# Four 32x32 blocks per head instead of two of 64x64 in the first levels of a triangular inverse

## The reference

```
up = jnp.einsum('bsnw,nwd->bsnd', branches, w_branch[l])
gates = jax.nn.sigmoid(gate_logits.reshape(b, s, N_BRANCH, D_MODEL))
x = x + jnp.sum(gates * up, axis=2) @ w_out[l]
```

## Time and profile before

| | |
|---|---|
| median of 3 runs | 2401.88 us |
| the runs | 2402.19, 2397.12, 2401.88 us |
| profiled execution | 2396.91 us |
| its span in the trace | 2395.1 us |
| PE busy | 2358.9 us, 98% |
| DVE, ACT, POOL busy | 989.7, 880.5, 1022.0 us |

### The profile page before, as it was taken

One profiled execution on the slowest core, in us unless ns is written; L12 is line 12 of the kernel. 1 busy time (PEld: TensorE's weight loads), 2 busy tenths in 40 slices (PEclk: granted clock), 3 DMA queues, 4 the chain that ended last, 5 costly groups with the idle time before them and its releaser, 6 DMA issues.

```text
span 2395.1 us, 35863 instructions
## 1 busy us (share of the span) xinstructions
PE 2358.9 (98%) x14266; PEld 1658.1 (69%) x14266; DVE 989.7 (41%) x1888; ACT 880.5 (37%) x1441; POOL 1022.0 (43%) x464
## 2 busy tenths in 40 slices
PE   8999999999999999999999999999999999999999
PEld 6744444444444444358889999888888889999887
DVE  5622222222222222245347865353453379653533
ACT  6411111101011101045447744544444477435443
POOL 0000000000000000028978555788889876547886
PEclk9999999999999999999999999999999999999999
DMA  8799999999999999945555433555555544335554
GB/s 300 298 429 429 429 429 429 430 430 430 430 429 430 430 430 430 428 183 194 193 178 168 136 125 120 171 190 192 190 179 192 189 156 154 127 101 182 176 192 143
DMA packets 96307, 650.92 MB, mean 272 GB/s; under 512 B 11088, under 2 KB 13560, under 8 KB 69688
## 3 DMA queue, kind: packets, MB, share of 16 engines
q1 hardware_dynamic: 96184, 649.21, 69.9%
HBM read 647.92 MB, written 1.25 MB: 271 GB/s over the span
## 4 chain that ended last, share of the span: by engine, by line
PE 87%; DMA 9%; DVE 3%; ACT 1%; issue 0%; POOL 0%; SPq 0%; DVEq 0%; ACTq 0%
PE bank L2477 22%; PE bank L924 12%; PE bank L669 11%; PE bank L671 10%; PE bank L670 10%; PE bank L925 6%; DMA ring<-in_expert_units 4%; DMA scratch<-in_expert_units 4%; PE bank L2464 4%; PE bank L2485 2%; PE bank L2828 1%; PE bank L2493 1%; PE bank L1418 1%; PE bank L1407 1%; PE bank L1364 0%
## 5 line engine op out<-in xcount | busy, mean ns | idle before, releaser
L656 POOL TENSOR_TENSOR w_lo<-raw,w_hi 128x1024 fp32r<-128x1024 f32 (+2 forms) x424 | 1010.5, 2412 | 1135.4 <-ACT w_hi L650 1135.2
L2477 PE MATMUL bank<-ring,scratch 128*64 128x512 f32 x2304 | 513.4, 596 | 8.8 <-DMA ring<-in_expert_units 8.8
L924 PE MATMUL bank<-hT_both,w_hi 128*128 128x512 f32 x1408 | 498.7, 398 | 4.5 <-DVE act_lo L1069 4.4
L650 ACT CAST w_hi<-raw 128x1024 fp32r<-128x1024 f32 (+2 forms) x424 | 421.6, 1041 | 180.2 <-PE bank L671 152.9
L925 PE MATMUL bank<-hT_both,w_lo 128*128 128x256 f32 x1408 | 395.1, 281 | 0.0
L2477 PEld LDWEIGHTS bank<-ring,scratch 128*64 128x64 f32 x2304 | 160.0, 137 | 323.2 <-issue 318.5
L924 PEld LDWEIGHTS bank<-hT_both,w_hi 128*128 128x128 f32 x1408 | 264.4, 188 | 70.7 <-DVE act_lo L1069 5.7
L2730 DVE TENSOR_TENSOR scratch<-bank,scratch 128x512 f32<-128x512 f32 x64 | 44.3, 692 | 597.8 <-PE bank L2493 593.8
L925 PEld LDWEIGHTS bank<-hT_both,w_lo 128*128 128x128 f32 x1408 | 266.0, 189 | 0.6
L2477 PE MATMUL bank<-scratch 128*64 128x512 f32 x768 | 172.3, 596 | 4.4 <-DMA scratch<-in_expert_units 3.3
L1058 DVE TENSOR_TENSOR bank<-bank,scratch 128x512 f32<-128x512 f32 x88 | 61.3, 697 | 275.0 <-PE bank L925 274.9
(11 more groups left out here) (388 smaller groups left out, 3326.9 us busy)
## 6 DMA issues: line engine op xcount, KB each, us to landing
ring<-in_expert_units SPq DMA_DIRECT2D x144, 2048.0 KB, 25.3
raw<-in_layer_halves SPq DMA_DIRECT2D x408, 512.0 KB, 3.8
scratch<-in_expert_units SPq DMA_DIRECT2D x47, 2048.0 KB, 26.3
ring<-in_first_units SPq DMA_DIRECT2D x11, 1024.0 KB, 11.0
ring<-in_ple_units SPq DMA_DIRECT2D x2, 2048.0 KB, 18.6
raw<-in_layer_halves SPq DMA_DIRECT2D x8, 424.0 KB, 3.2
raw<-in_layer_halves SPq DMA_DIRECT2D x4, 384.0 KB, 3.8
scratch<-in_expert_units SPq DMA_DIRECT2D x1, 1280.0 KB, 14.7
```

The lines of the kernel that those rows point to most:

```text
L650: k.nc.scalar.copy(k.w[0][i % SPLIT_SLOTS][:, at], k.raw[n % RAW_SLOTS][:, 0:at.stop - at.start]).then_inc(k.shared("weights_hi"), 1)
L656: k.nc.gpsimd.tensor_tensor(k.w[1][i % SPLIT_SLOTS][:, at], k.raw[n % RAW_SLOTS][:, 0:at.stop - at.start], k.w[0][i % SPLIT_SLOTS][:, at], ...
L924: nc.tensor.matmul(bank[:, :], w[0], both, start=start, stop=False)
L2477: last = nc.tensor.matmul(b[g * SL:(g + 1) * SL, :], lhsT[:, c, :], w[:, c, g, :], start=start and c == 0, stop=stop and c == 3)
```

## The change

Levels 0 to 4 need only diagonal blocks of 32x32: level 4 joins 16x16 blocks to 32x32. They now hold four such blocks per head (`BLOCK_ROWS`), as tiles of 128 partitions x 32 columns (`X_blocks`, `XT_blocks`, `P_blocks`). Level 4 writes its results block by block into the 64-column tiles, which DVE has set to zero before (`whole_zeros_dve`). Levels 5 and 6 are as they were. PE's list gets parts of the third gate's four quarters at other places: one in each of levels 1 to 5 between P and XP, one ahead of the last level, one inside it, one ahead of the tail; the tail's own five stay, and what is left (three parts) comes behind the tail.

```diff
+Q = 32
+BLOCK_ROWS = tuple(slice(r * Q, (r + 1) * Q) for r in range(4))
-def blocks_mm(nc, b, lhsT, rhs):
+def blocks_mm(nc, b, lhsT, rhs, blocks=HALF_ROWS):
+    n = P // len(blocks)
     for h in range(GH):
-        for rows in HALF_ROWS:
-            last = nc.tensor.matmul(b[rows, h * V:(h + 1) * V], lhsT(rows, h), rhs[rows, h, :], start=True, stop=True)
+        for rows in blocks:
+            last = nc.tensor.matmul(b[rows, h * n:(h + 1) * n], lhsT(rows, h), rhs[rows, h, :], start=True, stop=True)
...
-def level_pe(k, pe, lev):
+def level_operands(G, lev):
+    if lev < LEVELS - 2:
+        return G.X_blocks, G.XT_blocks, G.P_blocks, BLOCK_ROWS
+    return G.X, G.XT, G.P, HALF_ROWS
+
+def level_pe(k, pe, lev, fill):
     G, nc = Gdn(k), k.nc
+    X, XT, Pm, blocks = level_operands(G, lev)
     for t in range(NT):
         b, full = k.claim(pe, ("P", lev, t))
         k.evacuated(pe, ("X", t) if lev == 1 else ("XP", lev - 1, t))
-        blocks_mm(nc, b, lambda rows, h: G.m[rows, t, h, rows], G.X[:, t]).then_inc(full, 1)
+        blocks_mm(nc, b, lambda rows, h: G.m[rows, t, h, rows], X[:, t], blocks).then_inc(full, 1)
+    fill(1)
     for t in range(NT):
...
-def last_level_pe(k, pe):
+def last_level_pe(k, pe, fill):
     G, nc, (top, bottom) = Gdn(k), k.nc, HALF_ROWS
+    fill(1)
...
         last.then_inc(full, 1)
+    fill(1)
...
 def whole_zeros_dve(k, dve):
-    k.nc.vector.memset(Gdn(k).whole_XT[V:P, :, :, 0:V], 0.0)
+    G, V_ = Gdn(k), k.nc.vector
+    V_.memset(G.whole_XT[V:P, :, :, 0:V], 0.0)
+    V_.memset(G.X, 0.0)
+    k.evacuated(dve, ("QK", 0), ("QK", 1))
+    V_.memset(G.XT, 0.0).then_inc(k.sem("zeros_ready"), 1)
...
+    if lev == LEVELS - 3:
+        dve.wait_ge(*k.at("zeros_ready", 1))
+    for t in range(NT):
+        for key, old, wider in (("XP", X, G.X), ("PX", XT, (G.XT, G.whole_XT)[lev == LEVELS - 2])):
+            b, free = k.filled(dve, (key, lev, t))
+            step = part(b, GH, n)
+            if lev < LEVELS - 3 or (key == "XP" and lev == LEVELS - 2):
+                V_.tensor_tensor(old[:, t], old[:, t], step, ALU.subtract).then_inc(free, 1)
+                continue
+            for rows in blocks:
+                at = in_half(rows) if n == Q else rows
+                ins = V_.tensor_tensor(wider[rows, t, :, at], old[rows, t], step[rows], ALU.subtract)
+            ins.then_inc(free, 1)
...
-def tail_pe(k, pe, fillers):
+def tail_pe(k, pe, fill):
+    fill(1)
...
+    gate_quarters = chain(*[gates_pe(k, pe, 2, q) for q in range(4)])
...
     for lev in range(1, LEVELS - 1):
-        level_pe(k, pe, lev)
-    last_level_pe(k, pe)
-    whole(gates_pe(k, pe, 2, 0))
-    tail_pe(k, pe, [gates_pe(k, pe, 2, 1), gates_pe(k, pe, 2, 2), gates_pe(k, pe, 2, 3)])
+        level_pe(k, pe, lev, fill)
+    last_level_pe(k, pe, fill)
+    tail_pe(k, pe, fill)
+    whole(gate_quarters)
```

More of the change, by code:

```diff
@@ L74, in columns @@
     return out
-CONST = columns([("ident", P), ("ones", P), ("tri", P), ("after_mask", P), ("causal", 2 * P), ("levels", 6 * V), ("ident_halves", V), ("cos16", 32),
+CONST = columns([("ident", P), ("ones", P), ("tri", P), ("after_mask", P), ("causal", 2 * P), ("levels", 5 * Q), ("ident_blocks", Q), ("level5", V), ("cos16", 32),
                  ("sin16", 32), ("cos32", 64), ("sin32", 64), ("flip", P), ("tri_strict", P), ("iota", P), ("slot", P)])
@@ L1626, in lower_dve @@
     G, V_ = Gdn(k), k.nc.vector
[L1627 to L1631, removed]
+    first = k.c("levels")[:, 0:Q]
+    k.evacuated(dve, ("QK", 0), ("QK", 1))
+    for rows in BLOCK_ROWS:
+        ins = V_.tensor_tensor(G.XT_blocks[rows], G.m[rows, :, :, rows],
+                               bc(first[rows].unsqueeze(1).unsqueeze(1), [Q, NT, GH, Q]), ALU.mult)
     link(ins)
-    ident = bc(k.c("ident_halves").unsqueeze(1), [P, GH, V])
+    ident = bc(k.c("ident_blocks").unsqueeze(1), [P, GH, Q])
     for t in range(NT):
-        V_.tensor_tensor(G.XT[:, t], ident, G.XT[:, t], ALU.subtract).then_inc(k.sem("xt_ready"), 1)
+        V_.tensor_tensor(G.XT_blocks[:, t], ident, G.XT_blocks[:, t], ALU.subtract).then_inc(k.sem("xt_ready"), 1)
 def first_level_pe(k, pe):
     G, nc = Gdn(k), k.nc
-    ident = bc(k.c("ident_halves").unsqueeze(1), [P, GH, V])
+    ident = bc(k.c("ident_blocks").unsqueeze(1), [P, GH, Q])
     for t in range(NT):
@@ L1644, in first_level_pe @@
         pe.wait_ge(*k.at("xt_ready", t + 1))
-        blocks_mm(nc, b, lambda rows, h: G.XT[rows, t, h, :], ident).then_inc(full, 1)
+        blocks_mm(nc, b, lambda rows, h: G.XT_blocks[rows, t, h, :], ident, BLOCK_ROWS).then_inc(full, 1)
 def first_level_act(k, act):
@@ L1701, in level_dve @@
             k.evacuated(dve, ("XP", lev - 1, t))
-        V_.tensor_tensor(G.P[:, t], part(b, GH, V), mask, ALU.mult).then_inc(free, 1)
+        V_.tensor_tensor(Pm[:, t], part(b, GH, n), bc(mask.unsqueeze(1), [P, GH, n]), ALU.mult).then_inc(free, 1)
+    if lev == LEVELS - 3:
+        dve.wait_ge(*k.at("zeros_ready", 1))
     for t in range(NT):
[L1704 to L1712, removed]
+        for key, old, wider in (("XP", X, G.X), ("PX", XT, (G.XT, G.whole_XT)[lev == LEVELS - 2])):
[8 more added lines that the diff above has]
+            ins.then_inc(free, 1)
 def last_level_dve(k, dve):
@@ L1723, in last_level_dve @@
         V_.tensor_scalar(G.whole_XT[top, t, :, bottom], part(b, GH, V)[top], -1.0, None, ALU.mult).then_inc(free, 1)
-def tail_pe(k, pe, fillers):
[L1727 to L1731, removed]
+def tail_pe(k, pe, fill):
+    G, nc = Gdn(k), k.nc
+    fill(1)
     b, full = k.claim(pe, ("vn", 0))
@@ L3166, in layer_pe, with fill @@
     whole(branch_pe(k, pe, 0, 0), branch_pe(k, pe, 0, 1))
+    gate_quarters = chain(*[gates_pe(k, pe, 2, q) for q in range(4)])
+    def fill(quarters):
+        for _ in range(quarters):
+            next(gate_quarters, None)
     for lev in range(1, LEVELS - 1):
-        level_pe(k, pe, lev)
-    last_level_pe(k, pe)
-    whole(gates_pe(k, pe, 2, 0))
-    tail_pe(k, pe, [gates_pe(k, pe, 2, 1), gates_pe(k, pe, 2, 2), gates_pe(k, pe, 2, 3)])
+        level_pe(k, pe, lev, fill)
+    last_level_pe(k, pe, fill)
+    tail_pe(k, pe, fill)
+    whole(gate_quarters)
     k.evacuated(pe, ("oT", 1, 0), ("oT", 1, 1))
@@ L3509, in constants @@
         level = level.T if lev else level
-        levels.append(np.concatenate([level[0:V, 0:V], level[V:P, V:P]], axis=0))
+        if lev < LEVELS - 2:
+            levels.append(np.tile(level[0:Q, 0:Q], (P // Q, 1)))
+        else:
+            c["level5"] = np.tile(level[0:V, 0:V], (P // V, 1))
     c["levels"] = np.concatenate(levels, axis=1)
-    c["ident_halves"] = p % V == n[:, 0:V]
+    c["ident_blocks"] = p % Q == n[:, 0:Q]
     for half in (16, 32):
```

19 lines of the change are left out of this document (12 added, 7 removed).

## The result

The changed kernel takes 2411.27 us (median of 6 runs, 2410.16 to 2414.06); the kernel before took 2400.07 us in the same comparison (6 runs, 2396.82 to 2403.87). The ratio is 1.0052, with a 95% interval of 1.0041 to 1.0063. So it is slower by 0.5%, about 11 us; the forecast was 2413.5 us.

A forecast was written before the change was run, and what follows sets the result against it. PE bounds the kernel, and levels 1 to 4 would wait for program blocks of 256 instructions. 11.1 + 0 + 0.5 = 11.6 us on the profiled 2396.9 gives 2408.5, on the median 2413.5 us; range 2401 to 2424.

The forecast's parts named there:

- A block is 256 instructions, and one is fetched ahead: PE's program: the next block is asked for when one begins, so each costs at least 3.6 us whatever it holds.
- the stretch: PE from level 1's start to the tail's first product, eight gate parts inside: 36.9 us, +11.1 us over both layers.
- the first rival: Program arrives in time and DVE's chain alone holds PE in the levels: -0.4 to -7 us, 2395 us; chance 8%.
- The pace of a block: PE in levels 1 to 4: 4.1 us per 256 instructions, so level 4's issue ends after 23.7 us.
- the second rival: Blocks bind in levels 1 to 4 but near their floor of 3.6 us: +4.7 us, 2406.5 us; chance 16%.
- From there to the tail's first product: From the end of level 4's issue, through DVE's sixteen steps, level 5 and the last level: 13.2 us.
- Turns of 32 columns: Small products on PE: four row quarters work side by side, about 32 ns a turn, 8 ns per MATMUL.
- the third rival: Row quarters take turns on PE, a level with its part costs 7.9 us: +27 us, 2429 us; chance 4%.
- Level 0 and the memsets: Smaller level 0 products save 0.4 us per layer, two new memsets ahead of branch_dve cost 0.4: together 0.
- Behind the tail: Branch product 2 waits for ACT to empty gate quarter 2's bank: 0.25 us per layer, +0.5 us (0 to 3.2).
- The sum: Whole kernel: 11.1 + 0 + 0.5 = 11.6 us slower, 2413.5 us on the median; chance 72%.

The follow-up runs named there:

- blocks only: The changed kernel with the gate parts of levels 1 to 5 and of the last level put back ahead of the tail: 2418.65 us, ratio 1.0095.
- two parts a level: The changed kernel with two gate parts instead of one in each of levels 1 to 4: 2422.73 us, ratio 1.0098.
- half the heads: The changed kernel with the products of levels 0 to 4 formed for two of the four heads only: 2393.39 us, ratio 0.9974.
- the kernel of 64x64 with parts in levels 1 to 5: The kernel before, 64x64 blocks kept, with one part of the third gate in each of levels 1 to 5: 2395.21 us, ratio 0.9985.

## Why the prediction was right

**A block is 256 instructions, and one is fetched ahead: right.** Restarts of 126 and 127 MATMULs apart in the kernel with blocks only, eight packets in the stretch (seven or eight predicted), restarts 2.4 and 2.6 us after a packet began (1426.11 to 1428.48, 1438.04 to 1440.63; 2.3 predicted), once 3.5 (1429.83 to 1433.34, where the packet itself took 2.1); in layer 1 it is 2.4, 2.5 and 2.3. PE's waits for "issue" at these products are six of 1.6 us on the mean (0.5 to 2.1), instead of eight of 1 to 2. "One ahead" is what these distances fit; how many blocks PE can hold is not seen in a trace.

The Trainium skill (Runtime: NRT & Kernel Launch, Instruction fetch mechanics) calls the crossing of a block "mostly hidden". By the first rival, which rested on that, the time would have been 2395 us and the packets under 3 us apart. The ten restarts from "issue" in the kernel with blocks only, 21.9 us together, and the fall of those waits with the number of instructions, speak against it for products this small; in the dense stretch of the earlier trace rows it holds (PE busy for 75.50 of 75.50 us).

**The pace of a block: too slow by some 0.3 us.** The prediction took 4.1 us, a mean over four intervals of which one was long (5.7). The packets of layer 0 begin at 1426.11, 1429.83, 1434.44, 1438.04, 1441.84 and 1445.42: a mean of 3.9, four of the five within 3.6 to 3.8; in layer 1 the mean is 3.8 (3.5 to 4.1). The end of level 4's issue came 22.8 us after level 1's start in both layers (1422.65 to 1445.41), where the sum said 23.7 and the second rival, with 3.6 us a block, 21.2. So the pace lies between the two, and the end of issue nearer to the sum than to the rival.

**From there to the tail's first product: 15.7 and 15.2 us instead of 13.2.** (The terms that the prediction lists add up to 13.4.) Nothing else in the sum was off by so much. PE's second P of level 5 starts 3.0 us after the end of issue (1445.41 to 1448.42) instead of 2.1. That it waits for L1741 was right, and so was a step of DVE; DVE, changed kernel, layer 0:

```profile
1444.69 4.80 DVE L1741 TENSOR_TENSOR scratch<-scratch,bank 32x128 f32<-32x128 f32 x16 [2.97 <-PE bank L1423]
```

Sixteen steps in 4.80 us, 0.30 each (0.29 predicted). But DVE could begin only 0.7 us before PE was done, since PE's product that it waited for stood behind the last hole. Then the clock: this P takes 1.06 us to the next start instead of 0.47, and the gate part behind it 2.66 (1449.48 to 1452.14) instead of 1.8. With 9.0 us for the rest, as predicted, that is 15.7. In layer 1 the clock falls later, from 2120.8, and the same four terms are 2.6, 0.6, 2.4 and 9.7. The step that failed is the silent one: every duration was taken from rows at full clock, though the prediction itself put some eight holes of 1 to 2 us in front of them. Too slow a block (-0.9, -1.0) and the lost clock with the later start (+2.5, +2.0) cancel in part, so the stretch was 38.45 and 37.94 us against 36.9; +13.5 us against +11.1.

**Turns of 32 columns: right.** At full clock a batch of 64 MATMULs (level 0, the row at 1401.55) takes 0.57 us from the first start to the last, 9 ns each (8 predicted), where 64x64 takes 29 to 30. So the third rival falls: four quarters of the rows do work side by side. At half clock a batch takes 0.84 us, 13 ns each (layer 0, from 1443.90).

**Level 0 and the memsets: both small, one wrong.** Level 0 gave 0.39 us per layer, as said. The memsets cost nothing. From the old memset to the step that frees the bank it is 2.78 us (1412.64 to 1415.42) against 2.77 in the earlier trace rows, although two memsets of 0.48 came in between: the tiny step between them, which ran for 1.52 us in the kernel before, takes 0.44 behind them. Its length was a wait: in the kernel before it ends at 1413.98 and POOL's instruction (L656, the split of the weights) at 1413.95; in the changed kernel it ends at 1414.66 and POOL's at 1414.64. In each of the ten traces all such tiny steps of DVE (128x8 or 128x4) that ran over 0.4 us, 16 to 20 of them, end 0.01 to 0.03 us after an instruction of POOL. The memsets went into that wait, and so the prediction was wrong to add them. DVE, layer 0:

```profile
1412.64 0.48 DVE L1714 MEMSET scratch<- 64x512 f32 x1 [0.16 <-issue]
1413.28 0.48 DVE L1715 MEMSET scratch<- 128x512 f32 x1 [0.15 <-issue]
1413.82 0.48 DVE L1717 MEMSET scratch<- 128x512 f32 x1
1414.22 0.44 DVE L1790 TENSOR_TENSOR scratch<-scratch 128x8 f32<-128x8 f32 x1
...
1415.42 0.68 DVE L1898 SCALAR_TENSOR_TENSOR scratch<-scratch,bank 128x512 f32<-128x512 f32 x1
```

**Behind the tail: 0 instead of 0.5.** From the tail's first product to the transposes behind branch 2 it is 29.26 us against 35.03 before, which is just the four parts (5.76): no wait, in layer 1 either. The prediction gave a reason for little or no wait, that POOL would be through earlier, and it was right. Two tiny steps of DVE in the chain to ACT's start had waited for POOL in the kernel before; now POOL is through at 1467.6, ahead of them, and they take 0.16 and 0.17 us. POOL and DVE, layer 0, before and (last two rows) changed:

```profile
1458.94 5.18 POOL L656 TENSOR_TENSOR w_lo<-raw,w_hi 128x1024 fp32r<-128x1024 f32 x2 [5.50 <-ACT w_hi L650]
1460.27 1.51 DVE L1808 TENSOR_TENSOR scratch<-scratch 128x4 f32<-128x4 f32 x1
1461.81 2.33 DVE L1809 TENSOR_SCALAR scratch<-scratch 128x4 f32<-128x4 f32 x1
...
1474.44 0.16 DVE L1832 TENSOR_TENSOR scratch<-scratch 128x4 f32<-128x4 f32 x1
1474.64 0.17 DVE L1833 TENSOR_SCALAR scratch<-scratch 128x4 f32<-128x4 f32 x1
```

From DVE's vn to ACT's start it is 4.2 us (1472.39 to 1476.57) instead of the 7.7 that the prediction had read. Three parts are enough cover here; none is too few, as the kernel with two parts a level shows.

**The sum.** By the profiles, 13.5 - 0.8 = 12.7 us of the 14.2; by the medians, 11.2 us against 11.6 predicted. So part of the closeness is luck: the stretch was 2.4 us worse than predicted, level 0, the memsets and the tail 1.3 better, and the comparison of medians 1.5 kinder than the profiles' terms, within the spread of the runs. That the mean block was a little shorter than the one taken hid more of the lost clock.

## What to carry to other kernels

Before a product is cut into smaller ones, count PE's instructions, not the columns: here a block of 256 instructions (64 fp32 products) cost 3.5 to 3.9 us in most cases, and never less than 3.4, however little the array had to do, so that all that the array saved below some 14 ns an instruction was lost. Long matmuls put between the short ones pay where they make each block last longer than that, one part in each block rather than two in every other, and only as long as the place that they are taken from keeps its cover. A step that runs long in a trace may be waiting for another engine: look what ends with it before adding work ahead of it or a price behind it. When a forecast holds holes, price the work behind them at the lower clock as well.

## What the runs showed of the hardware

- Program comes late with the queues empty: the packet at 1438.04 was the only DMA packet in its half microsecond, and PE restarted 2.6 us after it began.
- Tiny steps of DVE ran until an instruction of POOL ended, 1.5 and 2.3 us instead of 0.16 (1460.27 and 1461.81 in the kernel before); the two ends lie 0.01 to 0.03 us apart in all ten traces.
- The granted clock falls to 1.2 GHz in a stretch with repeated holes of 1.7 to 2.1 us, although PE works between them: 0.87 and 0.82 on the mean of the stretches, 0.71 with holes of 1.4 to 3.4 us and no gate parts between. A gate matmul takes 0.21 us there instead of 0.12. In the kernel before, the three holes of 0.38 to 1.64 us left it at 1.00; with half the heads it fell at one wait of 1.7 us in each layer. Not every fall has a long hole ahead of it: in the kernel of 64x64 with parts in levels 1 to 5 it is at half from 1451.6, just behind the stretch, where PE's last two waits were 0.28 and 0.37 us. What decides it is not shown.
- Products of 32x32 in four quarters of the rows cost 9 ns per MATMUL as fp32, against 29 for 64x64 in two halves; a weight load goes with each, so by an estimate from these 9 ns PE could take a block of 256 instructions in 1.2 us, a third of the time in which the next one comes.
